# The second layer's modulations, moved from a stage of TensorE's into the first feed-forward's up projection, on VectorE

## The chip, the cores and the metric

The kernel runs on one core of one Trainium2 chip. The metric is the device time of one execution in microseconds (us); the number shown is the median of three runs. Engines are TensorE (PE in the profile, with PEld for its weight loads), VectorE (DVE), ScalarE (ACT), GpSimd (POOL) and SyncE (SP), which here only issues DMAs.

## The reference

Two blocks of a network over a sequence of 512 latent and 256 context tokens of width 1024, all float32. The first block has two layers; each begins with a modulation:

```python
def ada_mod(cv, w, b):
    m = jax.nn.silu(cv) @ w + b          # w: 1024 x 6144
    return jnp.split(m, N_MOD, axis=-1)  # N_MOD = 6
```

Six vectors of 1024 come out: shift, scale and gate for the layer's mixer and for its feed-forward. `cv` is `c` for the latent tokens and `c_ctx` for the context. In layer 0 both are used in full. In layer 1 the context tokens are needed only as keys and values of the attention, so of the context's six vectors only the mixer's shift and scale are read. Layer 0 is a convolution and an mLSTM mixer, then `conv_ffn`: `(silu(dwconv(g) + b) * u) @ w_down` with `g, u = split(h @ w_up)`, where `w_up` has 5632 columns. Layer 1 is latent attention (`mla`), then the same feed-forward. A second block with attention, a state space and a mixture of experts follows.

## The kernel before, in words

The program is a list of stages (`steps` in `build`, L3065 and on); each is a block with one program for each engine, and the next stage begins when all engines are through. In order: load, mod0, hyproj, hyena, mlstm, out0, **up0**, down0, **mod1**, mla, up1, down1, final, block2, moe. SBUF is one big area, cut anew by each stage. Activations lie as eight tiles of 128 channels by 768 tokens (`k.x`), for products also as a pair of a rounded high part and a low part, so that each product is three passes of TensorE (`three_passes`, L284 to L289).

*mod1* is `modulations(k, 1, k.mod_next)`. The weights lie in memory as 12 groups of 128 x (8 x 512): 2 MB each, 25 MB in all. SP loads them into three slots, a slot again when `done` says that TensorE is through with it (L502). For each group TensorE does eight products with `silu_c` (128 x 2, c and c_ctx) as the stationary side and 512 columns of weights moving (L511); VectorE copies the 2 x 512 result (L526), TensorE turns it with four small products (L516), and VectorE adds the bias into `mod_next` (L530). At the end `mixer_gains` makes `gain` = (scale + 1) x norm weight with four small operations (L479). `mod_next` is read from mla on; `gain` is one buffer for both layers.

*up0* is `ffn_up(k, 0, hidden, scratch, SEGS, ...)`. It first normalises: ScalarE squares, VectorE adds the squares (L352), TensorE sums over partitions with a 128 x 1 column of ones (L361), ScalarE takes the root, TensorE spreads it (L367), VectorE scales and ScalarE shifts. TensorE runs some unneeded products meanwhile (`keep_running`, L273). Then come 22 tiles of 128 hidden channels as 11 turns of two (p = 0, 1). `Stream` brings the weights: SP loads 1 MB into one of two raw buffers when `ready` says that it is free (L252 the first two, L257 the rest), ScalarE rounds it to the high part (L262), VectorE subtracts for the low part (L266). For a tile TensorE does 96 products (gate and up, over 512 and 256 tokens) into three of PSUM's eight banks, banks 0 to 2 for p = 0 and 3 to 5 for p = 1; it waits for `ready[p]` and `taken[p]` before and signals `product[p]` after. ScalarE waits for `product`, rounds the next weights of this p, puts the middle tap of the convolution into `scratch` (L769) and, after VectorE's two outer taps (L792, L798), applies SiLU (L772). VectorE does, in this order: the next weights' `low`, the outer taps, the product with `up` into `hidden` (L802), which signals `taken[p]`. GpSimd has nothing to do in up0 but to clear the semaphores of the stage before. Each engine works its program in the order in which it is written.

Of the kernel before, what the change touches and what calls it, by code (L numbers as in the profile page):

```python
# [31 lines left out]
P = 128  # L32
# [89 lines left out]
class Kernel:  # L122


    def __init__(self, nc, ctx, dram):
# [23 lines left out]
        self.y_rows = nc.dram_tensor("y_rows", (2 * LAT, D), F32, kind="Internal").ap()  # L149
        self.slot_list = nc.dram_tensor("slot_list", ((N_EXPERTS + 7) * P, 1), F32, kind="Internal").ap()  # L150
        self.back_in = [ctx.enter_context(nc.semaphore(f"back_in{s}")) for s in range(8)]
        self.ps = ctx.enter_context(nc.psum_tensor("ps", [P, 8 * BANK], F32))
# [147 lines left out]


def from_first(engine, turns, turn):

    turn(0, True)
    if turns > 1:
        with engine.Fori(1, turns) as i:
            turn(i, False)
# [101 lines left out]


def project_few(k, w, psum_of, segs, m):

    for s, (t0, n) in enumerate(segs):
        for kk in range(DT):
            for part, x in enumerate((k.h_pair.high_plain, k.h_pair.low_plain)):
                last = k.nc.tensor.matmul(psum_of(s), w[:, kk * m:(kk + 1) * m], x[:, kk, t0:t0 + n],
                                          start=kk == 0 and part == 0, stop=kk == DT - 1 and part == 1)
    return last
# [54 lines left out]

def mixer_gains(k, layer, mod):

    for a, norm in enumerate(("norm_mix", "norm_ffn")):
        w = COL[f"{norm}_{layer}"]
        for c in range(2):
            k.nc.vector.scalar_tensor_tensor(  # L479
# [231 lines left out]

def ffn_up(k, layer, hidden, scratch, segs, norm):
    nc = k.nc
    k.stage()
    norm = Norm(k, *norm, segs, k.pair(3), k.bank(6), 5)
    stream = Stream(k, f"ffn_up_{layer}", 2 * D)
    turns, ns = stream.tiles // 2, len(segs)
# [12 lines left out]
    with k.block() as block:  # L730
# [5 lines left out]
        def _(pe):  # L736
            norm.sum_and_spread(pe)

            def turn(i, first):
                for p in range(2):  # L740
# [3 lines left out]
                    up_of = lambda s: up(p)[:, segs[s][0]:segs[s][0] + segs[s][1]]  # L744
                    if first and p == 0:
                        project_as_normed(k, pe, norm, stream.parts[p], gate_of, segs, 0, 2 * P)
                    else:
                        project(k, stream.parts[p], DT, k.h_pair, gate_of, segs, 0, 2 * P)
                    project(k, stream.parts[p], DT, k.h_pair, up_of, segs, P, 2 * P).then_inc(product[p], 1)

            from_first(pe, turns, turn)

        @block.scalar
        def _(act):
# [19 lines left out]
            in_turns(act, turns, turn)  # L774

        @block.vector
        def _(dve):
            free_all(dve, taken)
            norm.add(dve)
            for p in range(2):  # L780
                stream.low(dve, p, 1)
            norm.scale(dve)

            def turn(i, last):
                for p in range(2):
                    n = 2 * i + p
                    if not last:
                        stream.low(dve, p, i + 2)
# [7 lines left out]
                    for a, w in segs:  # L796
# [5 lines left out]
                    nc.vector.tensor_tensor(hidden[:, n, t0:t1], scratch[:, p, t0:t1],  # L802
                                            up(p)[:, t0:t1], ALU.mult).then_inc(taken[p], 1)

            in_turns(dve, turns, turn)

# [2251 lines left out]
def build(nc, dram, out, upto=None):  # L3058
    with ExitStack() as ctx:
# [5 lines left out]
        def shift(a, layer=0):  # L3065
# [12 lines left out]
            ("out0", lambda: project_residual(k, "w_out_0", pair, 2, SEGS)),  # L3078
            ("up0", lambda: ffn_up(k, 0, hidden, scratch, SEGS, (gain(1), shift(1)))),
            ("down0", lambda: [ffn_down(k, "ffn_down_0", hidden, k.mod, seg) for seg in SEGS]),  # L3080
            ("mod1", lambda: modulations(k, 1, k.mod_next)),
            ("mla", lambda: mla(k, (gain(0), shift(0, 1)))),
# [168 lines left out]
```

## Time and profile before

| | us |
|---|---|
| median of 3 runs (lowest, highest) | 3586.95 (3586.47, 3593.13) |
| the profiled execution, its own time | 3593.25 |
| its span in the profile | 3591.5 |
| TensorE busy in it | 3091.0 (86%) |
| VectorE busy | 1596.9 (44%) |
| ScalarE busy | 1214.4 (34%) |
| GpSimd busy | 128.0 (4%) |
| TensorE's granted clock, mean | 0.926 of full speed |

Busy time is the time in which an engine has an instruction at work; TensorE's matmuls overlap, so its rows are longer than their distance from each other. A timeline row gives the start, the length, engine, line, operation, what it writes and reads, its count (several like instructions in a row are merged) and in brackets how long the engine was idle before it and what ended that. Granted clock is the share of full speed that TensorE's clock was given.

### The profile page before, as it was taken

What the parts mean: (1) busy time and instruction counts of PE and PEld (TensorE: products, weight loads), DVE (VectorE), ACT (ScalarE), POOL (GpSimd) and SP (SyncE); (2) the same over time, 40 slices, a digit from 0 to 9 for tenths busy, and PEclk for the clock granted to TensorE, in tenths of its full rate; (3) what the DMA queues carried; (4) which work ended last, traced back from release to release, by engine and by line L of the source; (5) the groups of instructions that cost most, each with busy time, mean ns of one, the idle gap of its engine ahead of it and who ended that gap; (6) DMA issues with size and microseconds to landing.
All of it is one profiled execution on the core that took longest, in us unless ns stands there. A gap on an engine that the chain in (4) does not pass through costs nothing. (4 is left out here: it accounts for less than half of the span.)

```text
span 3591.5 us, 38068 instructions
## 1 busy us (share of the span) xinstructions
PE 3091.0 (86%) x14423; PEld 2367.5 (66%) x14423; DVE 1596.9 (44%) x2100; ACT 1214.4 (34%) x1614; POOL 128.0 (4%) x83
## 2 busy tenths in 40 slices
PE   6896798888999999887799999978965788499997
PEld 2483377677888887265577788757753566477775
DVE  1343341544333343033464434342247644478886
ACT  0320031324332232033232444233423332277775
POOL 0000000200000000000000000000000100112120
PEclk9997899899999999998799999989987889699998
DMA  6211011011111132711001222211300012489996
GB/s 249 104 41 63 18 47 47 1 47 71 59 67 61 59 128 73 264 49 40 17 1 47 94 94 70 93 62 62 94 19 0 1 40 82 178 320 347 348 337 246
DMA packets 71122, 362.72 MB, mean 101 GB/s; under 512 B 12852, under 2 KB 16771, under 8 KB 43876
## 3 DMA queue, kind: packets, MB, share of 16 engines
q1 hardware_dynamic: 64132, 352.85, 27.6%
q0 software_dynamic: 6880, 8.41, 0.6%
q8 instruction: 67, 1.10, 0.1%
q14 instruction: 43, 0.35, 0.0%
HBM read 360.68 MB, written 16.27 MB: 105 GB/s over the span
## 5 line engine op out<-in xcount | busy, mean ns | idle before, releaser
L287 PE MATMUL ps<-rounded,rounded 128*128 128x512 f32 (+3 forms) x3700 | 1377.5, 372 | 108.2 <-DVE rounded L1867 23.7
L288 PE MATMUL ps<-rounded,rounded 128*128 128x512 f32 (+3 forms) x3700 | 1338.1, 362 | 0.0
L289 PE MATMUL ps<-rounded,rounded 128*128 128x512 f32 (+3 forms) x3700 | 1336.2, 361 | 0.0
L287 PEld LDWEIGHTS ps<-rounded,rounded 128*128 128x128 f32 (+1 forms) x3700 | 705.5, 191 | 286.6 <-issue 74.5
L289 PEld LDWEIGHTS ps<-rounded,rounded 128*128 128x128 f32 (+1 forms) x3700 | 706.6, 191 | 107.5
L288 PEld LDWEIGHTS ps<-rounded,rounded 128*128 128x128 f32 (+1 forms) x3700 | 707.9, 191 | 94.8
L266 DVE TENSOR_TENSOR rounded<-work,rounded 128x1024 fp32r<-128x1024 f32 (+3 forms) x224 | 306.6, 1371 | 941.8 <-ACT rounded L262 941.6
L262 ACT CAST rounded<-work 128x1024 fp32r<-128x1024 f32 (+3 forms) x224 | 260.8, 1166 | 691.4 <-PE ps L289 563.7
L3014 DVE TENSOR_TENSOR rounded<-work,rounded 128x2048 fp32r<-128x2048 f32 x138 | 311.7, 2288 | 90.8 <-ACT rounded L2862 88.4
L2862 ACT CAST rounded<-work 128x2048 fp32r<-128x2048 f32 x138 | 258.6, 1909 | 83.3 <-PE ps L289 83.3
L273 PE MATMUL ps<-cst 128*128 128x256 f32 x544 | 154.0, 447 | 102.0 <-PEq L168 102.0
L273 PEld LDWEIGHTS ps<-cst 128*128 128x128 f32 x544 | 121.4, 229 | 132.8 <-issue 112.5
L511 PE MATMUL ps<-work,silu_c 128*2 128x512 f32 x384 | 173.5, 606 | 24.1 <-DMA work<-in_ada_w 24.1
L511 PEld LDWEIGHTS ps<-work,silu_c 128*2 128x2 f32 x384 | 31.1, 86 | 145.1 <-issue 144.8
L343 ACT ACTIVATE h<-x 128x768 f32<-128x768 f32 (+1 forms) x40 | 26.5, 743 | 281.8 <-PEq L168 281.8
L262 ACT ACT_TABLE_LOAD x34 | 43.6, 1283 | 202.2 <-PE ps L289 194.2
L526 DVE COPY work<-ps 2x512 f32<-2x512 f32 x24 | 16.3, 679 | 181.3 <-PE ps L511 181.3
L702 DVE SCALAR_TENSOR_TENSOR work<-ps,vec,work 128x255 f32 (+4 forms) x116 | 72.5, 653 | 30.9 <-ACT work L674 24.9
L2307 POOL TENSOR_TENSOR h<-work,row 128x2048 f32<-128x2048 f32 x2 | 9.2, 4640 | 2144.7 <-DVE row L2389 2144.7
L772 ACT ACTIVATE work<-work 128x768 f32<-128x768 f32 (+1 forms) x44 | 32.5, 739 | 118.1 <-DVE work L798 118.1
L1867 DVE TENSOR_TENSOR rounded<-ps,rounded 128x768 fp32r<-128x768 f32 (+1 forms) x64 | 52.3, 818 | 42.7 <-ACT rounded L1834 42.7
L1861 DVE TENSOR_REDUCE row<-ps 128x1 f32<-128x768 f32 (+1 forms) x64 | 52.5, 820 | 27.4 <-PE ps L289 27.2
(428 smaller groups left out, 2528.2 us busy)
## 6 DMA issues: line engine op xcount, KB each, us to landing
work<-in_moe SPq DMA_DIRECT2D x138, 1024.0 KB, 7.1
work<-in_ada_w SPq DMA_DIRECT2D x24, 2048.0 KB, 8.0
work<-in_ffn_up SPq DMA_DIRECT2D x44, 1024.0 KB, 4.8
work<-in_ffn_down SPq DMA_DIRECT2D x66, 512.0 KB, 3.3
work<-in_w_out SPq DMA_DIRECT2D x16, 512.0 KB, 3.6
work<-in_w_gates SPq DMA_DIRECT2D x16, 512.0 KB, 3.6
work<-in_w_in_hy SPq DMA_DIRECT2D x12, 512.0 KB, 3.3
work<-in_hy_dft_lat SPq DMA_DIRECT2D x4, 1024.0 KB
```

What stands on the lines that cost most here:

```text
L262: self.k.nc.scalar.copy(self.parts[s][0], self.raw[s]).then_inc(self.rounded[s], 1)
L266: self.k.nc.vector.tensor_tensor(self.parts[s][1], self.raw[s], self.high_plain[s], ALU.subtract).then_inc(self.ready[s], 1)
L273: k.nc.tensor.matmul(k.bank(bank, 2 * P), k.const("ident"), k.cst[:, 0:2 * P], start=True, stop=True)
L287: k.nc.tensor.matmul(out, sh, mh, start=start, stop=False)
L288: k.nc.tensor.matmul(out, sh, ml, start=False, stop=False)
L289: return k.nc.tensor.matmul(out, sl, mh, start=False, stop=stop)
L511: last = nc.tensor.matmul(k.bank(s)[0:2, :], k.silu_c[:, kk, :], slots[s][:, kk * 512:(kk + 1) * 512], start=kk == 0, stop=kk == DT - 1)
L702: nc.vector.scalar_tensor_tensor(out=out, in0=k.pair(p)[:, lo + o:hi + o], scalar=k.col(conv_w, n + tiles * (o + taps // 2)), in1=out, op0 ...
L1861: chain.link(nc.vector.tensor_reduce(stats[:, b, 0:1], scores(u), AX.X, ALU.max))
L1867: nc.vector.tensor_tensor(turned_part(pair.low, u), turn_bank(u).rearrange("p (b q) -> p b q", q=P), turned_part(pair.high_plain, u), ALU. ...
L2862: nc.scalar.copy(ring.parts[:, c % ring.SPLIT, 0, :], ring.raw[c % ring.RAW]).then_inc(ring.rounded, 1)
L3014: V.tensor_tensor(ring.parts[:, s, 1, :], ring.raw[c % ring.RAW], ring.plain[:, s, 0, :], ALU.subtract).then_inc(ring.ready, 1)
```

## The change

The stage mod1 is gone. Its work is done in up0 by a new class, `Background`, whose parts are called from up0's engine programs in turns 1 to 9.

- The 6144 columns are 24 pairs of 128-column tiles. GpSimd loads each pair in two halves (4 of the 8 blocks of 128 rows each, 128 partitions x 4 runs of 1 KB, 512 KB), 48 loads into two buffers. Load n waits until load n - 2 is eaten.
- VectorE multiplies a 128 x 256 piece of the weights by the column of `silu_c` that belongs to it and adds it to a running sum in SBUF, for each of the eight blocks; the first is a plain product. The first 8 pairs are done for both vectors (turns 1 to 4, one pair in each tile: 16 operations), the other 16 pairs for c alone (turns 5 to 8, two pairs in each tile: 16 operations). Each step waits for the one before it.
- TensorE, one turn later (turns 2 to 9), sums over partitions: after a tile's own products, four matmuls with a 128 x 128 piece of a sum stationary and the column of ones moving, into bank 6 or 7. VectorE then copies the four columns (`keep`).
- Behind the last turn VectorE adds the bias for all of `mod_next` with two operations and makes three of the four gains; the fourth is not read by anything.
- The context's modulations of index 2 to 5 in layer 1, which nothing reads, are no longer made.
- The turns are written out as spans with a body each (`in_spans`): on TensorE turn 0, turn 1, 2 to 5, 6 to 9, and 10. up1 has no such part and works as before. The buffers lie where up0 has `hidden` tiles 19 to 21 (written from turn 9 on) and behind `scratch`.

```diff
--- before.py
+++ after.py
@@ -148,6 +148,7 @@
         self.h_rows = nc.dram_tensor("h_rows", (LAT, D), F32, kind="Internal").ap()
         self.y_rows = nc.dram_tensor("y_rows", (2 * LAT, D), F32, kind="Internal").ap()
         self.slot_list = nc.dram_tensor("slot_list", ((N_EXPERTS + 7) * P, 1), F32, kind="Internal").ap()
+        self.mod_landed = [ctx.enter_context(nc.semaphore(f"mod_landed{s}")) for s in range(2)]
         self.back_in = [ctx.enter_context(nc.semaphore(f"back_in{s}")) for s in range(8)]
         self.ps = ctx.enter_context(nc.psum_tensor("ps", [P, 8 * BANK], F32))
         self.n_stage, self.used = 0, 0
@@ -297,6 +298,15 @@
             last = three_passes(k, psum_of(s), [w[:, at:at + P] for w in parts], x.tokens(kk, t0, t0 + n),
                                 kk == 0, kk == kt - 1)
     return last
+
+
+def in_spans(engine, spans, turn):
+    for a, b, kind in spans:
+        if b == a + 1:
+            turn(a, kind)
+        elif b > a:
+            with engine.Fori(a, b) as i:
+                turn(i, kind)
 
 
 def from_first(engine, turns, turn):
@@ -406,6 +416,87 @@
             k.nc.vector.tensor_tensor(self.part(k.h_pair.low, kk), self.part(k.h, kk), self.part(k.h_pair.high_plain, kk),
                                       ALU.subtract).then_inc(self.ready, 1)
             scale(kk + 2)
+
+
+class Background:
+    UNITS, BOTH = 4, 2 * DT
+    PAIR = 2 * P
+
+    def __init__(self, k, layer, weights_at, sums_at):
+        self.k, self.layer, self.src = k, layer, k.dram[f"ada_w_{layer}"]
+        self.weights = [k.plain(weights_at + s * D, DT // 2, self.PAIR) for s in range(2)]
+        self.sums = [k.words(sums_at + u * self.PAIR, sums_at + (u + 1) * self.PAIR) for u in range(self.UNITS)]
+        self.line = k.words(sums_at + 4 * self.PAIR, sums_at + 4 * self.PAIR + 8 * DT)
+        self.landed = k.mod_landed
+        self.stepped = [k.sem("mod_stepped_two"), k.sem("mod_stepped_one")]
+        self.eaten, self.used, self.lined = (k.sem(s) for s in ("mod_eaten", "mod_used", "mod_lined"))
+
+    def fetch(self, pool):
+        for n in range(N_MOD * DT):
+            pair, half = n // 2, n % 2
+            if n >= 2:
+                pool.wait_ge(self.eaten, n - 1)
+            group = self.src[pair // 2].rearrange("p (k n) -> p k n", k=DT)
+            at = pair % 2 * self.PAIR
+            pool.dma_start(self.weights[half], group[:, 4 * half:4 * half + 4, at:at + self.PAIR]).then_inc(self.landed[half], 16)
+
+    def add(self, dve, p, q, vectors, landed, stepped, steps, eaten):
+
+        for kk in range(DT):
+            if kk % 4 == 0:
+                dve.wait_ge(self.landed[kk // 4], landed + 16)
+            if kk == 4:
+                dve.wait_ge(self.eaten, eaten + 1)
+            elif kk:
+                dve.wait_ge(stepped, steps + (kk if kk < 4 else kk - 1))
+            for c in range(vectors):
+                total, by, tile = self.sums[2 * p + q + c], self.k.silu_c[:, kk, c:c + 1], self.weights[kk // 4][:, kk % 4, :]
+                if kk == 0:
+                    done = self.k.nc.vector.tensor_scalar(total, tile, by, None, ALU.mult)
+                else:
+                    done = self.k.nc.vector.scalar_tensor_tensor(out=total, in0=tile, scalar=by, in1=total, op0=ALU.mult,
+                                                                 op1=ALU.add)
+            done.then_inc(self.eaten if kk % 4 == 3 else stepped, 1)
+
+    def add_for_both(self, dve, i, p):
+        self.add(dve, p, 0, 2, 32 * i + 16 * (p - 2), self.stepped[0], 12 * i + (6 * p - 12), 4 * i + (2 * p - 4))
+
+    def add_for_one(self, dve, i, p):
+        for q in range(2):
+            self.add(dve, p, q, 1, 64 * i + 16 * (2 * p + q - 12), self.stepped[1], 24 * i + (12 * p + 6 * q - 120),
+                     8 * i + (4 * p + 2 * q - 24))
+
+    def sum(self, pe, i, p, both):
+
+        k = self.k
+        pe.wait_ge(self.eaten, 4 * i + (2 * p - 6) if both else 8 * i + (4 * p - 28))
+        pe.wait_ge(self.lined, 2 * i + (p - 3))
+        for u in range(self.UNITS):
+            part, tile = (u % 2, u // 2) if both else (u // 2, u % 2)
+            k.nc.tensor.matmul(k.bank(6 + p, 1, u), self.sums[2 * p + part][:, tile * P:tile * P + P],
+                               k.cst[:, ONE:ONE + 1], start=True, stop=True).then_inc(self.used, 1)
+
+    def free(self, dve):
+        dve.sem_inc(self.lined, 2)
+
+    def keep(self, dve, i, p):
+        dve.wait_ge(self.used, 8 * i + (4 * p - 12))
+        self.k.nc.vector.tensor_copy(self.line[:, bass.ds(8 * i + (self.UNITS * p - 16), self.UNITS)],
+                                     self.k.bank(6 + p, self.UNITS)).then_inc(self.lined, 1)
+
+    def finish(self, dve, mod):
+        k, both = self.k, self.BOTH
+        dve.wait_ge(self.lined, 2 + 8 * DT // self.UNITS)
+        bias = k.vec[:, COL[f"ada_b_{self.layer}"]:COL[f"ada_b_{self.layer}"] + N_MOD * DT]
+        k.nc.vector.tensor_tensor(mod[:, 0:both, :], self.line[:, 0:2 * both].rearrange("p (j c) -> p j c", c=2),
+                                  bias[:, 0:both].unsqueeze(2).to_broadcast([P, both, 2]), ALU.add).then_inc(self.lined, 1)
+        k.nc.vector.tensor_tensor(mod[:, both:N_MOD * DT, 0], self.line[:, 2 * both:8 * DT], bias[:, both:N_MOD * DT],
+                                  ALU.add).then_inc(self.lined, 1)
+        dve.wait_ge(self.lined, 4 + 8 * DT // self.UNITS)
 
 
 def project_few(k, w, psum_of, segs, m):
@@ -471,11 +562,11 @@
             nc.scalar.activation(k.silu_c[:, :, 1], k.vec[:, COL["c_ctx"]:COL["c_ctx"] + DT], ACT.Silu)
 
 
-def mixer_gains(k, layer, mod):
+def mixer_gains(k, layer, mod, vectors=((0, 1), (0, 1))):
 
     for a, norm in enumerate(("norm_mix", "norm_ffn")):
         w = COL[f"{norm}_{layer}"]
-        for c in range(2):
+        for c in vectors[a]:
             k.nc.vector.scalar_tensor_tensor(
                 out=k.gain[:, a, :, c], in0=mod[:, (3 * a + 1) * DT:(3 * a + 2) * DT, c], scalar=1.0,
                 in1=k.vec[:, w:w + DT], op0=ALU.add, op1=ALU.mult)
@@ -709,10 +800,11 @@
 
 
 
-def ffn_up(k, layer, hidden, scratch, segs, norm):
+def ffn_up(k, layer, hidden, scratch, segs, norm, beside=None):
     nc = k.nc
     k.stage()
     norm = Norm(k, *norm, segs, k.pair(3), k.bank(6), 5)
+    next_mod, beside = beside, Background(k, 1, WORK_AT + 19 * T, WORK_AT + (FFT + 2) * T) if beside is not None else None
     stream = Stream(k, f"ffn_up_{layer}", 2 * D)
     turns, ns = stream.tiles // 2, len(segs)
     t0, t1 = segs[0][0], T
@@ -736,19 +828,21 @@
         def _(pe):
             norm.sum_and_spread(pe)
 
-            def turn(i, first):
+            def turn(i, kind):
                 for p in range(2):
                     pe.wait_ge(stream.ready[p], i + 1)
                     pe.wait_ge(taken[p], i + 1)
                     gate_of = lambda s: gate(p, *segs[s])
                     up_of = lambda s: up(p)[:, segs[s][0]:segs[s][0] + segs[s][1]]
-                    if first and p == 0:
+                    if kind == "first" and p == 0:
                         project_as_normed(k, pe, norm, stream.parts[p], gate_of, segs, 0, 2 * P)
                     else:
                         project(k, stream.parts[p], DT, k.h_pair, gate_of, segs, 0, 2 * P)
                     project(k, stream.parts[p], DT, k.h_pair, up_of, segs, P, 2 * P).then_inc(product[p], 1)
-
-            from_first(pe, turns, turn)
+                    if kind in ("sum both", "sum one"):
+                        beside.sum(pe, i, p, kind == "sum both")
+
+            in_spans(pe, ((0, 1, "first"),) + (((1, 2, ""), (2, 6, "sum both"), (6, 10, "sum one"), (10, turns, "")) if beside else ((1, turns, ""),)), turn)
 
         @block.scalar
         def _(act):
@@ -773,18 +867,25 @@
 
             in_turns(act, turns, turn)
 
+        if beside:
+            @block.gpsimd
+            def _(pool):
+                beside.fetch(pool)
+
         @block.vector
         def _(dve):
             free_all(dve, taken)
+            if beside:
+                beside.free(dve)
             norm.add(dve)
             for p in range(2):
                 stream.low(dve, p, 1)
             norm.scale(dve)
 
-            def turn(i, last):
+            def turn(i, kind):
                 for p in range(2):
                     n = 2 * i + p
-                    if not last:
+                    if kind != "last":
                         stream.low(dve, p, i + 2)
                     dve.wait_ge(middle, ns * (n + 1))
                     for a, w in segs:
@@ -801,8 +902,18 @@
                     dve.wait_ge(gated, n + 1)
                     nc.vector.tensor_tensor(hidden[:, n, t0:t1], scratch[:, p, t0:t1],
                                             up(p)[:, t0:t1], ALU.mult).then_inc(taken[p], 1)
-
-            in_turns(dve, turns, turn)
+                    if "keep" in kind:
+                        beside.keep(dve, i, p)
+                    if "both" in kind:
+                        beside.add_for_both(dve, i, p)
+                    if "one" in kind:
+                        beside.add_for_one(dve, i, p)
+
+            spans = ((0, 1, ""), (1, 2, "both"), (2, 5, "keep both"), (5, 9, "keep one"), (9, 10, "keep"), (10, turns - 1, ""))
+            in_spans(dve, (spans if beside else ((0, turns - 1, ""),)) + ((turns - 1, turns, "last"),), turn)
+            if beside:
+                beside.finish(dve, next_mod)
+                mixer_gains(k, 1, next_mod, ((0, 1), (0,)))
 
 
 
@@ -3076,9 +3187,8 @@
             ("hyena", lambda: hyena(k, k.area(0, 12, T))),
             ("mlstm", lambda: mlstm(k, pair)),
             ("out0", lambda: project_residual(k, "w_out_0", pair, 2, SEGS)),
-            ("up0", lambda: ffn_up(k, 0, hidden, scratch, SEGS, (gain(1), shift(1)))),
+            ("up0", lambda: ffn_up(k, 0, hidden, scratch, SEGS, (gain(1), shift(1)), k.mod_next)),
             ("down0", lambda: [ffn_down(k, "ffn_down_0", hidden, k.mod, seg) for seg in SEGS]),
-            ("mod1", lambda: modulations(k, 1, k.mod_next)),
             ("mla", lambda: mla(k, (gain(0), shift(0, 1)))),
             ("up1", lambda: ffn_up(k, 1, hidden, scratch, SEG_LAT, (gain(1), shift(1, 1)))),
             ("down1", lambda: ffn_down(k, "ffn_down_1", hidden, k.mod_next, SEG_LAT[0])),
```

## Rows read from the trace of the kernel before

**Rows 1.** Windows view, three stretches: length, busy us of each engine, PEclk, DMA share, GB/s.
```profile
822.80:1224.00 401.20, 385.25 (x2184) 337.73 (x2184) 142.42 (x162) 133.74 (x141) 0.00 (x0) 0.99 0.16 58
...
1434.30:1551.90 117.60, 98.96 (x288) 27.15 (x289) 10.54 (x28) 0.00 (x0) 0.00 (x0) 0.94 0.57 214
1050.00:1100.00 50.00, 50.00 (x289) 44.29 (x288) 16.32 (x18) 14.21 (x14) 0.00 (x0) 1.00 0.17 63
```

**Rows 2.** Timeline around mod1: start us, us, engine, line, op, count, [idle before it].
```profile
1428.67 5.36 DVE L870 SCALAR_TENSOR_TENSOR x<-ps,mod,x 128x512 f32<-128x512 f32 x8 [7.97 <-PE ps L289]
...
1434.30 1.29 SPq L498 DMA_DIRECT2D work<-in_ada_w  x3
...
1442.41 9.84 PE L511 MATMUL ps<-work,silu_c 128*2 128x512 f32 x16 [13.78 <-DMA work<-in_ada_w]
...
1551.21 0.40 DVE L479 SCALAR_TENSOR_TENSOR gain<-mod_next,vec 128x8 f32<-128x8 f32 x4
1551.86 0.81 SPq L252 DMA_DIRECT2D work<-in_mla_w_down  x2
```

**Rows 3.** Timeline, VectorE, in a middle turn of up0.
```profile
986.77 2.29 DVE L266 TENSOR_TENSOR rounded<-work,rounded 128x2048 fp32r<-128x2048 f32 x1 [8.71 <-ACT rounded L262]
...
992.43 0.95 DVE L802 TENSOR_TENSOR work<-work,ps 128x768 f32 x1 [1.02 <-ACT work L772]
1004.81 2.29 DVE L266 TENSOR_TENSOR rounded<-work,rounded 128x2048 fp32r<-128x2048 f32 x1 [11.43 <-ACT rounded L262]
...
1010.46 0.96 DVE L802 TENSOR_TENSOR work<-work,ps 128x768 f32 x1 [1.02 <-ACT work L772]
1020.13 2.29 DVE L266 TENSOR_TENSOR rounded<-work,rounded 128x2048 fp32r<-128x2048 f32 x1 [8.71 <-ACT rounded L262]
```

**Rows 4.** Timeline, ScalarE, the same turn.
```profile
1001.58 1.28 ACT L262 ACT_TABLE_LOAD   x1 [9.29 <-PE ps L289]
...
1018.19 1.91 ACT L262 CAST rounded<-work 128x2048 fp32r<-128x2048 f32 x1 [7.87 <-PE ps L289]
```

**Rows 5.** Timeline, TensorE, the column sums of a norm in mla.
```profile
1561.03 1.50 PE L361 MATMUL ps<-cst,row 128*128 128x1 f32 x12 [1.97 <-DVE row L352]
```

**Rows 6.** Timeline, VectorE operations with all operands in SBUF, up0 and down0.
```profile
825.53 6.27 DVE L352 TENSOR_TENSOR row<-row,h 128x768 f32<-128x768 f32 x6
...
1233.09 0.42 DVE L859 TENSOR_TENSOR rounded<-work,rounded 128x256 fp32r<-128x256 f32 x1
```

**Rows 7.** DMA view, issues: queue, count, KB each, median us from issue to landing.
```profile
work<-in_w_in_hy SPq DMA_DIRECT2D x12, 512.0 KB, 3.3
...
work<-in_mla_w_kn SPq DMA_DIRECT2D x8, 128.0 KB, 2.0
```

**Rows 8.** Timeline, GpSimd's indirect DMAs in moe: its part without and with VectorE beside it.
```profile
3113.99 0.99 POOL L2723 DMA_INDIRECT h<-h_rows,whole  x1 [0.31 <-issue]
...
3470.61 2.12 POOL L2723 DMA_INDIRECT x<-h_rows,whole  x1 [0.31 <-issue]
```

**Rows 9.** Line views of L2717 (512 B each) and L2723 (gathers), last lines.
```profile
DMA to landing us min/median/max: 2.1/2.3/2.5
...
DMA to landing us min/median/max: 6.7/9.9/11.4
```

**Rows 10.** Timeline, ScalarE and VectorE at the start of up0, and its first loads.
```profile
828.73 3.68 ACT L262 CAST rounded<-work 128x2048 fp32r<-128x2048 f32 x2
...
831.72 4.49 DVE L266 TENSOR_TENSOR rounded<-work,rounded 128x2048 fp32r<-128x2048 f32 x2
...
work<-in_ffn_up SPq DMA_DIRECT2D x4, 1024.0 KB, 5.8
```

**Rows 11.** Timeline, TensorE's warm-up matmuls at the start of down0 and of mla.
```profile
1224.12 6.42 PE L273 MATMUL ps<-cst 128*128 128x256 f32 x16 [5.80 <-PEq L168]
...
1551.91 7.14 PE L273 MATMUL ps<-cst 128*128 128x256 f32 x32 [1.28 <-PEq L168]
```


## The prediction

> **What bounds the kernel now.** I read the page's second part first: TensorE's tenths stand at 9 over most of the span, so time goes down only where TensorE idles, or where it does work that is not needed. Then the windows view of the two stages that the change touches. mod1 is a stage by itself, 117.6 us long; TensorE is busy in 99 us of it, VectorE in 10.5, ScalarE and GpSimd in none [rows 1]. up0 is the other kind: in a middle stretch of 50 us TensorE is busy in all 50 at granted clock 1.00, VectorE in 16.3, ScalarE in 14.2, GpSimd in none, the DMA engines at 0.17 [rows 1]. So up0 has room on every engine but TensorE. Third, the timeline at both seams of mod1. The last VectorE operation of down0 ends at 1434.03, SP issues mod1's first load at 1434.30, mod1's last gain ends at 1551.61 and SP issues mla's first load at 1551.86 [rows 2]. Each stage waits for the one before it, so nothing of mod1 lies beside other work: its length is on the path in full.
>
> Fourth, VectorE's and ScalarE's timelines inside one turn of up0. A turn (two tiles) takes 1020.13 - 986.77 = 33.36 us [rows 3], 16.68 us for a tile, TensorE's time alone. In a tile VectorE runs from the start of its `low` to the end of L802: 1011.42 - 1004.81 = 6.61 us, then it is idle for 8.71 or 11.43 us [rows 3]. L802 ends 1011.42 - 1001.58 = 9.84 us after the product that ScalarE waited for [rows 3, 4]. TensorE needs the banks again only when the tile after that is done. This idle time is where the additions go.
>
> **The change part by part.**
>
> *mod1 goes:* 1551.86 - 1434.30 = 117.56 us less [rows 2]. One seam between down0 and mla stays, as there is one on each side of mod1 now.
>
> *TensorE's sums, added:* 16 tiles (turns 2 to 9) each get four matmuls of a 128x128 f32 tile with one column, of the same form as L361. There 12 records stand for six such matmuls and take 1.50 us [rows 5], so four take eight records, 8 x (1.50 - 0.25)/11 = 0.91 us, where 0.25 is the length of the last record. With some 0.1 us for the changes of form at both ends I take 1.0 us a tile, on the engine that sets up0's time: +16.0 us. Bounds: 16 x 0.9 = 14.5 if they follow each other as there, and 16 x 8 x 0.44 = 56 if each waited out its own load and run (rival B).
>
> *VectorE's additions:* 256 operations, 16 in each tile of turns 1 to 8. No row has one of this kind on SBUF operands alone, but a 128x256 subtraction in SBUF takes 0.42 us [rows 6], and a chain where each waits for the one before has (6.27 - 0.96)/5 - 0.96 = 0.10 us between two [rows 6]; 0.54 us a step, loop registers included. In turns 1 to 4 (both vectors) only every second one is waited for: 8 x (0.42 + 0.54) = 7.7 us, with the copy from PSUM and its wait (0.3 us, an estimate from the same gap) 8.0 us, under the smaller gap of 8.71. Both half loads have had most of a tile to land. Cost nothing; the cover is VectorE's idle time. If the gap is overrun, what queues behind the additions on VectorE is the next `low` (for it ScalarE's cast has been ready) and then the conv of that tile, and TensorE waits for that tile's `taken` only.
>
> *Turns 5 to 8 (one vector, two pairs a tile)* are tighter. Four half loads are eaten per tile and two buffers exist, so loads 3 and 4 can be issued only when 1 and 2 are eaten. With L the time from "eaten" to "landed", four steps are 2.15 us, the second half of the first pair is eaten at 4.3, the last half can begin at 4.3 + L, and the tile's additions take B = 4.3 + L + 2.15 + 0.3 = 6.75 + L. TensorE's tile is then 16.68 + 1.0 = 17.68 us; VectorE keeps pace while B <= 17.68 - 6.61 = 11.07, and beyond that it falls back by the excess at each of eight tiles against a slack of 17.68 - 9.84 = 7.8 us. So the loss is 8 x (L - 4.32) - 7.8, nothing below L = 5.3. L is the unknown: no load in the trace is direct and issued by GpSimd. From below: small transfers of GpSimd land in 2.1 [rows 9]. From above: its gathers, whose rows are 4 KB, with a full DMA queue beside them, 9.9 in the middle and 11.4 at most [rows 9]. The nearest row is SP's 512 KB load, 3.3 us [rows 7], plus GpSimd's own part, 0.99 us with VectorE waiting [rows 8], plus an allowance of 0.4 for its runs of 1 KB where SP's are of 4 (SP's 128 KB loads, in runs of 1 KB, take 2.0 [rows 7], so the runs alone cost little): L = 4.7, B = 11.4, fallen back 8 x 0.38 = 3 us in all, inside the slack. Cost 0; bounds 0 (L = 2.1) and 8 x 5.58 - 7.8 = 37 us (L = 9.9).
>
> The Trainium skill's page "DMA: Bandwidth & Descriptors", section "Anatomy of one DMA — SWDGE (gpsimd) path", fits such a load with 2.0 us plus its bytes over 436 GB/s; an estimate from that page is 3.2 us for 512 KB, and B would be 10 us. No run here shows one alone; by either price the sum is the same.
>
> *Start of up0:* GpSimd's first two loads (1 MB) now share the engines with the stream's first two of 1 MB, which land 5.8 us after issue in the middle [rows 10]. 1 MB at that rate is about 2.5 us; the second cast ends at 832.41, VectorE's second `low` at 836.21 [rows 10], and the cast may slip 2.6 us before `low` follows it at once, which leaves 1.3 us on the norm's chain. Bounds 0 and 2.6; I take +1.3.
>
> *End of up0:* two adds and three gains behind the last L802. Four gains took 0.40 us [rows 2]; with two waits +0.8 us.
>
> *Start of mla:* TensorE's granted clock. After a pause of 5.8 us, 16 warm-up records take 6.42 us (0.40 each), and mla's 32, right behind mod1, take 7.14 (0.22 each) [rows 11]. mla's will now follow a pause like the former. The eight 512-column matmuls of mod1, which began after 13.8 us of pause, took 9.84 us for 16 records [rows 2], 3 us more than at the later pace, so the low level (1.2 GHz) lasts some 6 us: 15 records at 0.40, 17 at 0.22, 9.8 us, where the sums are due at 1561.03 - 1551.91 = 9.1. +0.7 us, bounds 0 and 3.7 (all 32 at the low level).
>
> Sum: -117.6 + 16.0 + 0 + 0 + 1.3 + 0.8 + 0.7 = -98.8 us. The profiled execution took 3593.25 us (span 3591.5); less 98.8 that is 3494.5. It lies 6.3 us above the median of the runs, 3586.95, and the stages touched are no longer in one than in the other that I can see, so I take the change off the median: 3586.95 - 98.8 = 3488 us.
>
> **The rivals.**
>
> *A: the loads set the pace of turns 5 to 8.* L is 6 to 9.9 us. For it: GpSimd's own part takes 2.12 us, not 0.99, while VectorE works beside it [rows 8], which alone gives L = 5.8 and a loss of 4 us; the buffers are two only; and runs of 1 KB are short. Against: the gathers' 9.9 us came with the queue full at all times, here the DMA share is 0.17 [rows 1]. At L = 7 the loss is 13.6, at 9.9 it is 37: 3502 to 3525 us. The skill's page "SBUF — State Buffer", section "SBUF: two separate sides", states that GpSimd can't write descriptors while VectorE runs an operation in a two-port mode; here only the first product of each pair could be one, so by it L grows by one 0.42 us step at the most. The row with 2.12 beside other operations says that there is more to it, or less; no run here separates them.
>
> *B: TensorE's sums drain its pipeline.* Each of eight records costs its weight load and its run in full, 0.44 us, 56 us instead of 16: 3528 us. Against it: rows 5 show the same form back to back.
>
> *C: slower than before.* One mechanism: a half load of GpSimd takes so long that VectorE, in order, holds the `low` and the conv behind it, and TensorE waits at every tile of turns 5 to 8. It has to lose 98.8 us, so 8 x (L - 4.32) - 7.8 > 98.8, L > 17.6 us, half as much again as the longest gather, 11.4 [rows 9]. At L = 20 it is 3606 us.
>
> *D: the removed stage returns.* Something that mod1 hid (code loading, mla's first weights) is due in mla instead. The weights are loaded by mla itself, after the seam, in both; I see at most a few us, 3490 to 3500 us.
>
> **How the numbers follow.** The forecast, 3488 us with its own range 3479 to 3500 (D in it), gets 0.65; A 0.25; B 0.05; C 0.02; the rest is what I have not seen. The range is 3479 to 3520 us: its lower end is the sum with TensorE's additions at 14.5 and no small terms, 3484, less 5 us for D with the other sign (a seam less to fetch code for), its upper one A with L = 9. The range leaves out B, C and the worst of A. A measurement here can't tell less than about 0.2% (7 us) from no change: faster 0.96, same 0.02, slower 0.02.
>
> **What would show it.** mla's first load some 99 us earlier with down0 as long as now; up0 longer by about 18 us, spread evenly as 1.0 us a tile over turns 2 to 9; eight records of the new line in each of these tiles at 0.11 us spacing; VectorE idle for loads about 2.5 us a tile in turns 5 to 8, but TensorE never waiting on `taken`. Rival A shows as TensorE idle in turns 7 and 8 only, since the slack goes first. The prediction is wrong if TensorE idles in turns 1 to 4, or if an addition takes over 0.6 us from start to start.

## Result, and the profile after

The changed kernel takes 3493.74 us in the middle of four runs (3485.01 to 3495.09), the one before 3586.71 us in four runs beside it: ratio 0.9729, with a 95% interval of 0.9701 to 0.9756, as in all brackets behind a ratio below. A second set of six runs gave 3497.55 against 3589.9 us: 0.9754 (0.9723 to 0.9785). So it is 92 to 93 us faster. The forecast was 3488 us, 98.8 less. The profiled executions shown below took 3485.01 us (span 3483.2) after and 3593.25 before, 108.2 apart; 14.2 us of that lie in mla's attention alone (200.3 and 186.1 us). There TensorE's granted clock was 0.50, its low level of 1.2 GHz, over some 20 us before, and 1.00 in that part after; a second trace of the same changed program has 195.3 us for this stage. So I compare stage by stage, not span by span.

First the stages, by SP's timeline (the first load of a stage marks its start), for up0 of the kernel before and then for the changed kernel, and the windows view of the new up0 and of a middle stretch of turns 5 to 8 (length, busy us of each engine, PEclk, DMA share, GB/s):

```profile
822.82 0.82 SPq L252 DMA_DIRECT2D work<-in_ffn_up  x2
...
1224.07 0.82 SPq L252 DMA_DIRECT2D work<-in_ffn_down  x2
```

```profile
827.07 0.81 SPq L253 DMA_DIRECT2D work<-in_ffn_up  x2
...
1243.25 0.81 SPq L253 DMA_DIRECT2D work<-in_ffn_down  x2
...
1452.97 0.82 SPq L253 DMA_DIRECT2D work<-in_mla_w_down  x2
```

```profile
827.07:1243.25 416.18, 399.73 (x2312) 351.97 (x2312) 256.35 (x439) 133.73 (x141) 36.23 (x48) 0.99 0.34 116
1054.00:1104.00 50.00, 50.00 (x300) 44.67 (x299) 36.47 (x67) 13.36 (x13) 8.98 (x12) 1.00 0.51 167
```

up0 is 1243.25 - 827.07 = 416.18 us, where it was 1224.07 - 822.82 = 401.25: 14.9 more. down0 is 209.7 (210.2 before), and mla begins where down0 ends: the 117.56 us of [rows 2] are gone. In the middle stretch TensorE is busy in all 50 us as in [rows 1], VectorE in 36.5 instead of 16.3. The stages touched give 117.6 - 14.9 + 0.5 = 103 us less, and 102 with the slower start of mla (0.8 us, below).

TensorE between two tiles of up0 (VectorE is in turn 5 here), and GpSimd's loads in the DMA view (queue, count, KB each, median us from issue to landing):

```profile
1061.66 0.39 PE L290 MATMUL ps<-rounded,rounded 128*128 128x512 f32 x1
1061.89 0.95 PE L480 MATMUL ps<-cst,work 128*128 128x1 f32 x8
1062.70 0.37 PE L288 MATMUL ps<-rounded,rounded 128*128 128x256 f32 x1
```

```profile
work<-in_ada_w POOLq DMA_DIRECT2D x48, 512.0 KB, 4.1
```

The eight records of the sums follow the tile's products and are followed by the next tile's without a pause. Now VectorE in the same stretch, one tile of turn 5, and the groups by line and form (busy us, mean ns, idle before them and until what):

```profile
1071.17 0.95 DVE L903 TENSOR_TENSOR work<-work,ps 128x768 f32 x1 [1.02 <-ACT work L866]
1072.05 0.15 DVE L488 COPY work<-ps 128x4 f32 x1
1072.12 0.34 DVE L459 TENSOR_SCALAR work<-work,silu_c 128x256 f32<-128x256 f32 x1
1072.50 3.61 DVE L461 SCALAR_TENSOR_TENSOR work<-work,silu_c 128x256 f32<-128x256 f32 x7
1078.50 0.35 DVE L459 TENSOR_SCALAR work<-work,silu_c 128x256 f32<-128x256 f32 x1 [2.39 <-DMA work<-in_ada_w]
1078.89 1.52 DVE L461 SCALAR_TENSOR_TENSOR work<-work,silu_c 128x256 f32<-128x256 f32 x3
1081.26 2.05 DVE L461 SCALAR_TENSOR_TENSOR work<-work,silu_c 128x256 f32<-128x256 f32 x4 [0.85 <-DMA work<-in_ada_w]
1083.37 2.29 DVE L267 TENSOR_TENSOR rounded<-work,rounded 128x2048 fp32r<-128x2048 f32 x1
```

```profile
L461 DVE SCALAR_TENSOR_TENSOR work<-work,silu_c 128x256 f32<-128x256 f32 x224 | 103.7, 483 | 14.1 <-DMA work<-in_ada_w 8.2
...
L459 DVE TENSOR_SCALAR work<-work,silu_c 128x256 f32<-128x256 f32 x32 | 10.4, 347 | 18.2 <-DMA work<-in_ada_w 18.2
```

The tile's additions take 1083.3 - 1072.0 = 11.3 us, two waits for loads of 2.39 and 0.85 us among them, and the next `low` follows at once, where [rows 3] had 8.71 or 11.43 us of idle time before it. VectorE has no room left in turns 5 to 8: its `low` starts lie 17.84 and 17.69 us apart (1065.53, 1083.37, 1101.06) where TensorE's tiles are 17.58 apart, so it falls back by 0.1 to 0.3 us a tile. That stays inside the slack, the time until TensorE needs the banks again, and the waits view of up0 has no wait of TensorE for `taken`.

### The profile page after: what moved, and what is told of

Read it like the earlier page. It is cut to its first block and busy times, and to the rows that moved or that the text cites. A ratio compares the mean times of both kernels' runs of the same rounds, so it can differ in the third digit from the quotient of the medians.

```text
span 3483.2 us, 38114 instructions
## 1 busy us (share of the span) xinstructions
PE 3002.3 (86%) x14263; PEld 2349.5 (67%) x14263; DVE 1699.8 (49%) x2349; ACT 1214.2 (35%) x1614; POOL 164.8 (5%) x131
## 5 line engine op out<-in xcount | busy, mean ns | idle before, releaser
L461 DVE SCALAR_TENSOR_TENSOR work<-work,silu_c 128x256 f32<-128x256 f32 x224 | 103.7, 483 | 14.1 <-DMA work<-in_ada_w 8.2
L602 PE MATMUL ps<-work,silu_c 128*2 128x512 f32 x192 | 87.1, 608 | 10.9 <-DMA work<-in_ada_w 10.9
L866 ACT ACTIVATE work<-work 128x768 f32<-128x768 f32 (+1 forms) x44 | 32.5, 739 | 130.6 <-DVE work L899 130.6
L602 PEld LDWEIGHTS ps<-work,silu_c 128*2 128x2 f32 x192 | 15.6, 86 | 71.7 <-issue 71.5
```

The lines of the kernel that those rows point to most:

```text
L461: done = self.k.nc.vector.scalar_tensor_tensor(out=total, in0=tile, scalar=by, in1=total, op0=ALU.mult, op1=ALU.add)
L602: last = nc.tensor.matmul(k.bank(s)[0:2, :], k.silu_c[:, kk, :], slots[s][:, kk * 512:(kk + 1) * 512], start=kk == 0, stop=kk == DT - 1)
```

## The experiments

All are timed against the kernel before in the same session. A time of up0 is from its first load to down0's, in one trace of each kernel. Lines left out of a code cut are marked with `...`.

**The changed kernel again**, unchanged.

> The changed kernel once more, in five rounds, for a narrower ratio and a second trace. Theory 1 (the stages touched account for all: mod1 117.6 less, up0 14.9 more, down0 and the start of mla within 1): about 102 us less than before, ratio 0.9715. Theory 2 (something outside these stages gives 9 us back, as the first medians suggest, 93 us less): ratio 0.974, and the same stages outside up0 and mod1 are longer in this trace too.

Measured: 3497.55 us, ratio 0.9754 (0.9723 to 0.9785), up0 416.2. That is 92 us less, not the 102 of theory 1; theory 2 holds, and the stages named in the last two experiments are long in this trace too.

**The stage left out, nothing in its place.**

```diff
-            ("mod1", lambda: modulations(k, 1, k.mod_next)),
+            nc.vector.memset(k.mod_next[:, :, :], 0.25)      # in load_inputs
```

> The kernel before with its stage mod1 left out and nothing in its place; mod_next is filled with a constant in the first stage. It leaves out all modulations of layer 1. Theory 1: 117.6 us less than before, 116.9 with the colder start of mla, so 3470 us, ratio 0.9674, and up0 is 401.2 us as before. Theory 2 (the removed stage hid something that comes back): less than 110 us are won, and the loss shows in a stage outside up0.

Measured: 3473.16 us against 3589.9, 116.7 less, ratio 0.968 (0.9654 to 0.9706); up0 401.2. mod1 was on the path in full, as the seams said. Nothing that it hid comes back: within the interval all of its 117.6 us are won, and of the stages behind it mla's first q stage (14.2 us) and z (29.0) are no longer than before (14.3 and 30.6).

**No sums on TensorE.**

```diff
-        dve.sem_inc(self.lined, 2)
+        self.k.nc.vector.memset(self.line, 0.25).then_inc(self.lined, 2)
 ...
-                    if kind in ("sum both", "sum one"):
-                        beside.sum(pe, i, p, kind == "sum both")
 ...
-                    if "keep" in kind:
-                        beside.keep(dve, i, p)
```

> The changed kernel without TensorE's sums over partitions and without VectorE's copies of them; the modulations of layer 1 are then constants plus bias. GpSimd's loads and VectorE's additions all stay. Theory 1 (the sums are all that up0 pays): up0 from 416.2 to 401.8 us, its length before plus 0.6 for the last operations, 14.4 us less than the changed kernel. Rival (the additions or the loads cost time themselves): up0 stays above 405 us. With 16.68 us a tile instead of 17.58 VectorE has less room: B is 11.3 against 16.68 - 6.6 = 10.1, 1.2 us too much at each of eight tiles, 9.6 us against a slack of 6.8, so 0 to 3 us of loss at the end of turn 8 are part of theory 1.

Measured: 3483.22 us, 14.3 less than the changed kernel; ratio 0.9713 (0.969 to 0.9737). up0 is 404.6 us, 11.6 less than in the changed kernel; in these traces the z stage of the second block, which the edit does not touch, is also 3.4 us shorter (29.1 against 32.5), so the total says more than up0 gained. The 404.6 are 401.2, 0.6 for its last operations, and 2.8 that the expectation had as VectorE's lateness in shorter tiles. The waits view shows 2.1 of them (who waited for whom, us, times, longest):

```profile
PE ps L288 <- DVE work L901: 2.1, 3, 1.0
```

So the sums cost 14.4 us (401.25 + 14.4 + 0.56 = 416.2), and the additions and loads nothing while TensorE's tile is 17.6 us long; at 16.7 they cost up to 2.8.

**Twice the additions in turns 5 to 8.**

```diff
+            if kk == 0 and vectors == 1:
+                dve.wait_ge(self.eaten, eaten)
 ...
-            for c in range(vectors):
-                total, by, tile = self.sums[2 * p + q + c], ...
+            for c in range(2):
+                total, by, tile = self.sums[2 * p + q + c] if c < vectors else self.spare, ...
```

> The changed kernel with 16 more operations of VectorE in each tile of turns 5 to 8: every piece is also multiplied by the second column and added to a spare sum that nothing reads. Loads and TensorE's sums as before. My model of the pace: 8 steps of a pair at 0.87 us, first pair 7.0 us, the third half load lands 4.5 us after the first is eaten, which is inside that time, so B = 14.0 + 0.3 = 14.3 us where 11.0 are free; 3.3 too much at eight tiles, 26 us, less a slack of 7.8: up0 18 us longer than the changed kernel's 416.2, 434 us, with TensorE idle only from turn 6 on. Rival (VectorE has more or less room than the model says, for example since ScalarE must follow it): 0 or over 30 us.

Measured: 3521.81 us against 3591.33, ratio 0.9791 (0.9744 to 0.9839), 70 us less where the changed kernel was 92 less; up0 441.2, 25 more than the changed kernel's, not 18. TensorE waits 16.7 us for `taken` (7 waits), where it had none. The timeline of a tile shows where the expectation was short:

```profile
1099.36 0.15 DVE L491 COPY work<-ps 128x4 f32 x1
1099.43 0.60 DVE L462 TENSOR_SCALAR work<-work,silu_c 128x256 f32<-128x256 f32 x2
1100.07 6.38 DVE L464 SCALAR_TENSOR_TENSOR work<-work,silu_c 128x256 f32<-128x256 f32 x14
1107.36 0.62 DVE L462 TENSOR_SCALAR work<-work,silu_c 128x256 f32<-128x256 f32 x2 [0.91 <-DMA work<-in_ada_w]
1108.02 6.49 DVE L464 SCALAR_TENSOR_TENSOR work<-work,silu_c 128x256 f32<-128x256 f32 x14
1114.43 2.28 DVE L267 TENSOR_TENSOR rounded<-work,rounded 128x2048 fp32r<-128x2048 f32 x1
```

The first half load is eaten some 3.4 us after the tile's first operation (1099.43), and the third, which goes into its buffer, can be used only at 1107.36, 7.9 us after that operation and not within the 7.0 that the pair takes. B, the time of a tile's additions, is 15.0 here and 15.9 in the next tile. With 15.5 the model gives 8 x (15.5 - 11.0) - 7.8 = 28 us, so with B taken from the trace it is good to a few us.

**One load in flight.**

```diff
-            if n >= 2:
-                pool.wait_ge(self.eaten, n - 1)
+            if n >= 1:
+                pool.wait_ge(self.eaten, n)
```

> The changed kernel with one of GpSimd's loads in flight at a time: load n waits until load n - 1 is eaten. VectorE then waits for three loads in each tile of turns 5 to 8 and for one in turns 1 to 4. From eaten to landed is 4.4 us in the trace, a half is 2.0 us of additions: B = 4 x 2.0 + 3 x 4.4 + 0.15 = 21.4 us where 11.0 are free, 10.4 too much at eight tiles, 83 us, less the slack left, 4 to 8: up0 75 to 79 us longer, 493 us, and the kernel within 30 us of the one before. In turns 1 to 4 B is 11.4: 3 us of the slack. This is what my rival C would look like at a third of its price. Rival (TensorE does not wait for VectorE's lateness this way): up0 under 450 us.

Measured: up0 495.7 us, 79.5 more; 3574.14 us against 3591.33, ratio 0.9943 (0.9918 to 0.9968): most of the gain is gone, 17 us are left of 92. VectorE waits three times in a tile, and TensorE now waits eight times for `taken`, 40.8 us in all, and eight times for the additions that its sums read, 17.9 us. The former in the waits view:

```profile
1142.12 0.34 DVE L459 TENSOR_SCALAR work<-work,silu_c 128x256 f32<-128x256 f32 x1
1142.50 1.53 DVE L461 SCALAR_TENSOR_TENSOR work<-work,silu_c 128x256 f32<-128x256 f32 x3
1148.40 2.05 DVE L461 SCALAR_TENSOR_TENSOR work<-work,silu_c 128x256 f32<-128x256 f32 x4 [4.37 <-DMA work<-in_ada_w]
1154.87 0.35 DVE L459 TENSOR_SCALAR work<-work,silu_c 128x256 f32<-128x256 f32 x1 [4.42 <-DMA work<-in_ada_w]
1155.26 1.52 DVE L461 SCALAR_TENSOR_TENSOR work<-work,silu_c 128x256 f32<-128x256 f32 x3
1162.08 2.05 DVE L461 SCALAR_TENSOR_TENSOR work<-work,silu_c 128x256 f32<-128x256 f32 x4 [5.29 <-DMA work<-in_ada_w]
```

```profile
PE ps L288 <- DVE work L903: 40.8, 8, 5.6
```

This is the mechanism of rival C at a smaller price, and it works as the prediction said: what queues behind the waiting addition is `low` and the conv, and TensorE pays once the slack is used up. The waits are 58.7 of the 79.5 us. The rest is no idle time: TensorE's granted clock over up0 was 0.91 here and 0.99 in the changed kernel, and its products were busy for 422 us instead of 400.

**The weights transposed: no part for TensorE.** One output column to a partition, 1024 inputs along the row, `silu(c)` and `silu(c_ctx)` spread over all partitions by ScalarE in turn 0:

```diff
+    pool.dma_start(self.weights[n % 2], self.src[n]) ...
 ...
+    nc.vector.scalar_tensor_tensor(out=..., in0=self.weights[b], scalar=1.0, in1=self.rows[c],
+                                   op0=ALU.mult, op1=ALU.mult, accum_out=mod[:, bass.ds(at, 1), c])
 ...
+    d["ada_t_1"] = np.ascontiguousarray(a["ada_w_1"].T.reshape(N_MOD * DT, P, D))
```

> A version meant to be faster: the weights of layer 1 lie transposed (48 tiles, 128 output columns on the partitions, 1024 inputs along the row), GpSimd loads them as 48 contiguous loads of 512 KB, VectorE multiplies a tile by the row of silu(c), which lies on all partitions, and adds along the row in the same instruction. TensorE has no part in it. Theory 1 (of the cost in up0 only the sums are left, and with them gone nothing is): up0 at 402 us, 14.4 less than the changed kernel, about 3479 us, ratio to before 0.970. VectorE: 4 operations of 1.2 us in a tile, 5 us instead of 7 to 11. Rival (loads of GpSimd or SBUF traffic disturb the stream): up0 above 405 us.

Measured: 3472.27 us (3462.26 to 3486.93), ratio 0.9687 (0.966 to 0.9714); up0 401.8. It is 25 us below the changed kernel in the same session, 14.4 of them in up0, and within 1 us of the kernel that does not make these modulations at all. Some 8 of the other 11 us lie in stages that neither version touches (q and k 1.9, v 1.0, z 3.9, the gates behind z 1.3 us, by the two traces), so only the 14.4 are shown to be its merit. Of all kernels here that make these modulations it is the fastest. One tile of turn 5 in its timeline:

```profile
1074.85 1.22 DVE L453 SCALAR_TENSOR_TENSOR work<-work 128x1024 f32<-128x1024 f32 x1
1075.99 0.08 DVE L453 DVE_READ_ACCUMULATOR work<-work  x1
1075.99 1.22 DVE L453 SCALAR_TENSOR_TENSOR work<-work 128x1024 f32<-128x1024 f32 x1
1077.14 0.08 DVE L453 DVE_READ_ACCUMULATOR work<-work  x1
1079.99 1.23 DVE L453 SCALAR_TENSOR_TENSOR work<-work 128x1024 f32<-128x1024 f32 x1 [2.77 <-DMA work<-in_ada_t]
1081.14 0.08 DVE L453 DVE_READ_ACCUMULATOR work<-work  x1
1082.24 1.22 DVE L453 SCALAR_TENSOR_TENSOR work<-work 128x1024 f32<-128x1024 f32 x1 [1.02 <-DMA work<-in_ada_t]
1083.39 0.08 DVE L453 DVE_READ_ACCUMULATOR work<-work  x1
1084.93 2.29 DVE L267 TENSOR_TENSOR rounded<-work,rounded 128x2048 fp32r<-128x2048 f32 x1 [1.46 <-ACT rounded L263]
```

Four operations of 1.22 us, each followed by 0.08 us that read its sum, replace sixteen of 0.35 to 0.48, and VectorE is idle again before its `low`, in spite of tiles of 16.7 us.

**Where the rest goes: the code before with other code in its place.** Two runs, on the stages that the change does not touch.

```diff
-            from_first(pe, turns, turn)
+            in_spans(pe, ((0, 1, True), (1, 2, False), (2, 6, False), (6, 10, False), (10, turns, False)), turn)
```

> Still open: stages that the change does not touch are longer in each trace of the changed kernel. From the stage's first load to the next stage's: the projection of q and k (before up0!) 78.9 to 79.0 us against 77.0, the one of v and its successor 45.7 against 44.8, mla's first q stage 15.8 against 14.3, the z stage of the second block 32.5 against 29.0 to 30.5; in the kernel without mod1 and without the additions they are as before. A stage that runs before up0 can only differ by where the program's code or data lie. This run is the kernel before with nothing changed but the code: up0's TensorE turns are written out as the five bodies that the changed kernel has (0, 1, 2 to 5, 6 to 9, 10); it does the same work. Theory A (the place of TensorE's code decides): the q and k stage takes 78.9, z 32.5, and the kernel 4 to 9 us more than before, ratio 1.001 to 1.0025. Theory B (something else, as the code of VectorE or GpSimd): 77.0 and 30.5, ratio 1.000.

Measured: the stage of q and k takes 548.68 - 469.68 = 79.0 us (77.0 before), the one after the next, v's, 45.7 (44.8), both as in the changed kernel. The other half of theory A failed: mla's first q stage stays at 14.4, and z took 29.1 where 32.5 was expected and the kernel before has 30.6. In all 3595.73 us against 3589.47, ratio 1.001 (0.9992 to 1.0027): the interval holds both no change and 9 us, so the total decides nothing. The start of the q and k stage, windows and timelines, of the kernel before and then of this one:

```profile
467.67:471.67 4.00, 3.69 (x16) 2.96 (x16) 0.00 (x0) 0.74 (x1) 0.00 (x0) 1.00 0.72 259
471.67:479.67 8.00, 6.39 (x39) 5.80 (x40) 2.45 (x2) 1.35 (x2) 0.00 (x0) 1.00 0.43 136
...
470.93 1.04 ACT L262 CAST rounded<-work 128x1024 fp32r<-128x1024 f32 x1 [47.44 <-DMA work<-in_w_in_qk]
...
473.28 0.39 PE L287 MATMUL ps<-rounded,rounded 128*128 128x256 f32 x1 [1.87 <-DVE rounded L266]
```

```profile
469.68:473.68 4.00, 3.69 (x16) 2.96 (x16) 0.00 (x0) 0.29 (x1) 0.00 (x0) 1.00 0.70 255
473.68:481.68 8.00, 5.93 (x31) 5.57 (x32) 2.45 (x2) 1.80 (x2) 0.00 (x0) 0.79 0.44 138
...
473.39 1.04 ACT L262 CAST rounded<-work 128x1024 fp32r<-128x1024 f32 x1 [47.99 <-DMA work<-in_w_in_qk]
...
475.75 0.39 PE L287 MATMUL ps<-rounded,rounded 128*128 128x256 f32 x1 [2.33 <-DVE rounded L266]
```

The first load is used 3.71 us after the stage's start and not 3.26; TensorE, behind its warm-up products, idles 2.33 us and not 1.87; and its clock is granted at 0.79 over the next 8 us and not at 1.00: a part of them at the low level, 1.2 GHz. The 0.45 us cost 2: an estimate from these rows is 0.45 + (1.00 - 0.79) x 8 = 2.1 us. All ten traces here fall into these two groups. The seven with five or six TensorE bodies in up0 have 3.58 to 3.85 us and 0.79 (the changed kernel 3.62 and 3.75, with pauses of 2.23 and 2.36); the kernel before, the stage left out and the transposed version have 3.18 to 3.39 us and 1.00.

```diff
-            ... (6, 10, "sum one"), (10, turns, "") ...
+            ... (6, 8, "sum one"), (8, 10, "sum one"), (10, turns, "") ...
```

> The changed kernel with the span of turns 6 to 9 on TensorE cut in two, 6 to 7 and 8 to 9: one body of code more, the same work. Theory A (the place of TensorE's code decides whether the first loads of some stages land a few tenths late): at least one of the four stages named above changes by more than 1 us against the changed kernel's 78.9, 45.7, 15.8 and 32.5, up0 stays at 416.2. Theory B: all four as in the changed kernel, total 3494 to 3498 us.

Measured: z 30.7 us (32.5 and 32.7 in the changed kernel), q and k 79.1, mla's q stage 15.9, up0 416.2; 3497.18 us. One of the four moved by more than 1 us, as theory A asks, and the total did not move beyond noise. So a change of TensorE's code alone moves some of these starts; that it is the place of the code, and why a load can then be used only later, is not shown.

The traces say more of the two other stages. z takes 28.8 to 29.1 us where the granted clock from 4 to 12 us behind its start was 1.00 (the stage left out, no sums, transposed, five bodies), 30.6 and 30.7 at 0.79 (before, one body more), and 32.5 to 33.1 at 0.61 to 0.64 (the changed kernel twice, twice the additions, one load in flight). So z was not at its best before either. mla's first q stage takes 14.2 to 14.4 us in the three kernels that add nothing in up0 and 15.8 to 15.9 in the other seven, the transposed version with no part for TensorE among them; behind the same pause of 13.95 us its 16 warm-up products take 5.1 to 5.3 us in the former and 6.7 in the latter. So neither TensorE's sums in up0 nor its five bodies are needed for it; which part of the new work makes these products slower there stays open.

## Why the prediction was right, by its steps

- *mod1, -117.56:* the trace says the same, and the stage left out gives 116.7 with the slower start of mla.
- *TensorE's sums, +16.0:* 14.4. A turn of two tiles went from 33.36 to 35.16 us, 0.90 a tile; the eight records come at the distance of [rows 5], and the 0.1 for changing the form was not there. Rival B is out.
- *Additions in turns 1 to 4, 0:* right; sixteen operations took 7.0 us, forecast 7.7.
- *Turns 5 to 8, 0 within 0 to 37:* right. L was 4.5 us (eaten at about 1074.0, next operation at 1078.50), taken as 4.7; B was 11.3, forecast 11.4. A step was 0.52 us from start to start as sized (0.54), though the operation itself takes 0.48 and the subtraction it was sized by 0.42: the wait between them is 0.04, not 0.10. Rival A is out at this L. No run has a larger one; the run with one load in flight shows its mechanism, loads that set VectorE's pace, at about the same L (4.3 to 4.6, once 5.3) with three waits in a tile. GpSimd's own part was 0.75 us with VectorE beside it, under both rows of [rows 8]; what slowed the gathers there did not act here. None of the 48 was issued during a first product (0.35 us each), so the part of rival A that rests on such a product was not tested. The estimate of 3.2 us for a load, worked out from the fit on the Trainium skill's page "DMA: Bandwidth & Descriptors", section "Anatomy of one DMA — SWDGE (gpsimd) path", compares with a median of 4.1 us from issue to landing here; contiguous 4 KB rows, in the transposed version, took 3.5. The measurement decides.
- *Start of up0, +1.3:* 0. The step was mis-sized in its last part, the 1.3 us on the norm's chain. ScalarE's second cast did wait 1.00 us for its load, but VectorE was still adding squares and took both `low` one after the other, as in [rows 10]:

```profile
835.87 1.90 ACT L263 CAST rounded<-work 128x2048 fp32r<-128x2048 f32 x1 [1.00 <-DMA work<-in_ffn_up]
...
835.96 4.48 DVE L267 TENSOR_TENSOR rounded<-work,rounded 128x2048 fp32r<-128x2048 f32 x2
```

- *End of up0, +0.8:* 0.56, from the last L903 (ends 1242.43) to the last gain (1242.99).
- *Start of mla, +0.7:* 0.8. The 32 warm-up records take 10.11 us, forecast 9.8, and the sums start 9.94 after them, not 9.12 [rows 5, 11]:

```profile
1453.03 10.11 PE L274 MATMUL ps<-cst 128*128 128x256 f32 x32 [5.72 <-PEq L169]
1462.97 1.40 PE L371 MATMUL ps<-cst,row 128*128 128x1 f32 x12
```

So the terms in these stages came to 102 us instead of 98.8, and 92 to 93 were measured. The difference is a term that the prediction does not have: stages that the change does not touch became longer. It is not rival D, whose mechanism was that something which mod1 hid is due in mla; the stage left out shows nothing of the kind. The places that stand in both traces of the changed kernel, against the profile of before, are q and k +2.0, v +0.9, mla's q +1.5, z +2.1, and the gates behind z +1.6: some 8 us. All but up0, mod1 and mla's attention took 2872 us in the trace of before, 2881 and 2883 in the two of the changed kernel, 2875 with the stage left out and 2873 transposed. This fits, but single executions scatter as much (up to 2891 in other kernels here), so the sum is no proof of each place. The number 3488 was near 3494 to 3498 partly by luck: two misses, 3 us too dear in up0 and 9 us not seen elsewhere, have opposite signs.

## What to carry to other kernels

Work of a stage of its own can be moved beside a stage that one engine fills, at the price of what it still asks of that engine; count what is free for the others from the row of idle time in one tile, and count the slack against the buffer's next use, because an in-order engine that is late costs nothing until that is spent. If a sum over partitions is all that is left for the busy engine, turn the weights so that the sum runs along the row. When a change of code is judged to a few tenths of a per cent, compare stages that it does not touch too.

## What the runs showed of the hardware that was not expected

- Adding TensorE code in one stage, with the same work done, made the first load of another, earlier stage usable 0.45 us later and that stage 2 us longer: TensorE's pause of 2.3 us instead of 1.9 was followed by a granted clock of 0.79 over 8 us instead of 1.00. The length of the pause alone does not tell: in the z stage a pause of 2.38 us was followed by 1.00 (five bodies) and one of 2.39 by 0.79 (one body more).
- A multiplication of two 128 x 1024 float32 tiles in SBUF with its sum along the row took 1.22 us and 0.08 for reading the sum.
- GpSimd's own part of a direct load of 512 KB took 0.75 us in the middle of 48, with VectorE's additions beside many of them; its part of an indirect one in moe took 0.99 and 2.12 us [rows 8].
